# Sparse attention on one Trainium2 core: transposes in pairs, products with the values two groups behind, and a third place for cache pages

## What is computed

```python
# for each of 8 query heads (2 key heads g x 4 r), three softmaxes over their own keys
s_c = q . kc * scale + bias(rel_c);  p_c = masked_softmax(s_c);  o_c = p_c @ vc     # compressed blocks of 32 keys
imp = p_c.sum(heads of g) per block of 64;  idx = top_k(imp + forced, 16)            # which blocks are read
s_s = q . ks[idx] * scale + bias(rel_s);     p_s = masked_softmax(s_s);  o_s = p_s @ vs   # selected blocks
s_w = q . k * scale + bias(rel), window 512; p_w = masked_softmax(s_w);  o_w = p_w @ v    # window
o = gate_0 * o_c + gate_1 * o_s + gate_2 * o_w
```

## Time and profile before

| | us |
|---|---|
| median of 3 runs | 2830.55 |
| lowest, highest | 2830.36, 2838.09 |
| profiled execution, its own time | 2830.92 |
| profiled execution, span of its instructions | 2829.3 |
| PE busy in the span | 2645.5 (94%) |
| DVE, ACT, POOL busy | 1318.7, 856.8, 703.0 |
| granted clock of PE, mean | 0.958 |

### The profile page before, as it was taken

The page is one execution under the profiler, slowest core; times in us unless marked ns, Lnnn a source line. Parts: engine busy times, 40 slices in busy tenths (PEclk is TensorE's granted clock), DMA queues, the critical chain, the costliest instruction groups (busy, mean ns, idle before and its releaser), DMA issues. The chain is left out here.

```text
span 2829.3 us, 52704 instructions
## 1 busy us (share of the span) xinstructions
PE 2645.5 (94%) x21842; PEld 2424.8 (86%) x21842; DVE 1318.7 (47%) x2314; ACT 856.8 (30%) x1606; POOL 703.0 (25%) x554
## 2 busy tenths in 40 slices
PE   8999999999889987788879999999999999999997
PEld 8999999989767764455559899988999999999996
DVE  6999999213133456455553352334233323323234
ACT  5332202113222324565652222134221121120222
POOL 2222222222243420111203424201422222222222
PEclk9999999999877887999989999999999999999998
DMA  5122353332376625334316551233111111111112
GB/s 185 48 66 69 99 106 87 96 99 68 121 257 222 205 94 183 126 116 152 122 66 210 150 179 61 75 134 136 49 43 49 47 46 45 46 45 45 45 45 69
DMA packets 149345, 290.33 MB, mean 103 GB/s; under 512 B 28356, under 2 KB 97160, under 8 KB 146354
## 3 DMA queue, kind: packets, MB, share of 16 engines
q1 hardware_dynamic: 137586, 255.49, 28.5%
q0 software_dynamic: 11520, 31.47, 3.5%
HBM read 245.94 MB, written 51.93 MB: 105 GB/s over the span
## 5 line engine op out<-in xcount | busy, mean ns | idle before, releaser
L147 POOL TENSOR_TENSOR mlp_w_low<-mlp_w_raw,mlp_w_high 128x1024 fp32r<-128x1024 f32 x72 | 173.6, 2411 | 649.4 <-ACT mlp_w_high L143 649.4
L371 PE MATMUL in_psum<-x_high,in_w_high 128*128 128x352 f32 x1416 | 266.7, 330 | 21.4 <-DVE x_low L566 11.4
L147 POOL TENSOR_TENSOR in_w_low<-in_w_raw,in_w_high 128x1024 fp32r<-128x1024 f32 x59 | 147.9, 2506 | 546.8 <-ACT in_w_high L143 546.8
L2815 PE MATMUL mlp_psum<-mlp_in,mlp_w_high 128*128 128x352 f32 x1536 | 264.9, 324 | 0.0
L143 ACT ACTIVATE mlp_w_high<-mlp_w_raw 128x1024 fp32r<-128x1024 f32 x72 | 76.4, 1061 | 621.5 <-PE mlp_psum L2815 621.5
L371 PEld LDWEIGHTS in_psum<-x_high,in_w_high 128*128 128x128 f32 x1416 | 237.5, 192 | 29.6 <-issue 15.1
L371 PE MATMUL in_psum<-x_low,in_w_high 128*128 128x352 f32 x1416 | 260.3, 325 | 0.0
L371 PE MATMUL in_psum<-x_high,in_w_low 128*128 128x352 f32 x1416 | 259.6, 325 | 0.0
L2815 PEld LDWEIGHTS mlp_psum<-mlp_in,mlp_w_high 128*128 128x128 f32 x1536 | 251.2, 189 | 0.2
L371 PEld LDWEIGHTS in_psum<-x_low,in_w_high 128*128 128x128 f32 x1416 | 236.2, 190 | 0.0
L371 PEld LDWEIGHTS in_psum<-x_high,in_w_low 128*128 128x128 f32 x1416 | 235.4, 190 | 0.0
(11 more groups left out here) (483 smaller groups left out, 4439.9 us busy)
## 6 DMA issues: line engine op xcount, KB each, us to landing
mlp_w_raw<-in_w_mlp SPq DMA_DIRECT2D x64, 512.0 KB, 3.6
in_w_raw<-in_w_in SPq DMA_DIRECT2D x59, 512.0 KB, 4.2
nsa_ring<-in_cache_slc SPq DMA_DIRECT2D x144, 128.0 KB, 4.0
gdnp_page_ring<-in_cache_cmp POOLq DMA_DIRECT2D x128, 128.0 KB, 4.9
gdnp_page_ring<-in_cache_cmp SPq DMA_DIRECT2D x128, 128.0 KB, 5.8
u_scratch<-stage SPq DMA_DIRECT2D x28, 528.0 KB, 5.3
nsa_ring<-in_cache_slc POOLq DMA_DIRECT2D x112, 128.0 KB, 4.1
aux<-u_scratch SPq DMA_DIRECT2D x24, 528.0 KB, 3.9
```

Source lines behind the costliest of these rows:

```text
L147: self.nc.gpsimd.tensor_tensor(self.low[:, i % 2, 0:k * P], self.raw[:, i % 2, 0:k * P], self.high[:, i % 2, 0:k * P].bitcast(F32), ALU.su ...
L371: return mm(psum[:, e % 2, n, 0:WN], w[:, i % 2, c * P:(c + 1) * P], a[:, c, n * WN:(n + 1) * WN], start=x == 0 and c == 0, stop=x == 2 an ...
L2815: return mm(psum[:, e % 2, n, 0:WN], w[:, i % 2, c * P:(c + 1) * P], a(c)[:, column(n)], start=x == 0 and c == 0, stop=x == 2 and c == CHU ...
```

## The change

It touches only the sparse stage.

- The turned groups have two PSUM banks (`TBANKS` 2, banks 4 and 5) and still three slots in SBUF (`TSLOTS` 3). The result regions are two (`REGIONS` 2), each in a bank of its own (6 and 7).
- A piece of the tail is now two groups of an item: both are turned, then the values follow of all groups up to two behind the last one turned (`BEHIND`). A single group at an item's end is a piece of its own. The values so run over an item's end into the next item; ahead of loop step 6 (`RANKED`), which uses the result banks for the samples' block flags, and at the end of the loop they are brought up in full.
- ACT copies a result when the copy of the second group after the item's last one is done (`keep_result`), and no more at the item's end.
- DVE's `biases(i)` waits until item i - 4 is turned, and no more for its result.
- The ring has three places. The third lies over the tiles of the block ranking (3 of 4 samples) and over early constants (the fourth). Set j waits for the item of set j - 3; set 2, the first in the third place, for the end of the ranking (`flags_ready`).

```diff
-    HB, SETS, FIRST_SET = NB // 2, 2, 4
+    HB, SETS, FIRST_SET = NB // 2, 3, 4
-    SLOTS, TBANKS, REGIONS, LAG = 4, 3, 4, 3
+    SLOTS, TSLOTS, TBANKS, REGIONS, LAG = 4, 3, 2, 2, 3
+    BEHIND = 2
+    place_of_group = [(i, k) for i in range(NI) for k in range(len(groups(i)))]
+    ends_item = {first_group[i + 1] - 1: i for i in range(NI)}
...
-        pt = S("probs_t", [P, TBANKS, 4, P])
+        pt = S("probs_t", [P, TSLOTS, 4, P])
...
-        ring = alias("ring", [P, SETS, HB, 4, 2 * PAGE])
+        ring = alias("ring", [P, 2, HB, 4, 2 * PAGE])
+        third = nc.alloc_sbuf_tensor_at("nsa_ring_third", [P, HB - 1, 4, 2 * PAGE], F32, offset=ranking_at)
+        third_last = nc.alloc_sbuf_tensor_at("nsa_ring_third_last", [P, 4, 2 * PAGE], F32, offset=early.at)
+        set_pages = lambda j, b: ring[:, j % SETS, b] if j % SETS < 2 else third[:, b] if b < HB - 1 else third_last
...
-        O_BANK, M0, M1 = 7, 6, 7
-        region = lambda i: ps[:, O_BANK, i % REGIONS * P:(i % REGIONS + 1) * P]
+        O_BANK, M0, M1 = 6, 6, 7
+        region = lambda i: ps[:, O_BANK + i % REGIONS, 0:P]
...
             elif j == 0:
                 eng.wait_ge(v_turned, 2)
+            elif j == 1:
+                eng.wait_ge(spilled, 16)
             else:
-                eng.wait_ge(spilled, 16)
+                eng.wait_ge(flags_ready, 1)
...
-            def tail(i, step):
-                n = len(groups(i))
-                if step < n:
-                    turn(i, step)
-                if step >= 1:
-                    values(i, step - 1)
+            valued = [0]
+
+            def values_up_to(end):
+                while valued[0] < end:
+                    values(*place_of_group[valued[0]])
+                    valued[0] += 1
...
                 if i == RANKED:
+                    values_up_to(first_group[i - LAG])
                     pe.wait_ge(flags_ready, 1)
...
-                tailing = [(i - LAG, s) for s in range(len(groups(i - LAG)) + 1)] if i >= LAG else []
+                tailing = [(i - LAG, s) for s in range(0, len(groups(i - LAG)), 2)] if i >= LAG else []
                 for which, (n, k) in merged(scoring, tailing):
-                    (tail if which else score)(n, k)
+                    if which:
+                        pair = range(k, min(k + 2, len(groups(n))))
+                        for one in pair:
+                            turn(n, one)
+                        values_up_to(first_group[n] + pair[-1] + 1 - BEHIND)
+                    else:
+                        score(n, k)
+            values_up_to(first_group[NI])
...
                     next(exp_parts, None)
+                    if G - BEHIND in ends_item and ends_item[G - BEHIND] != RANKED - LAG - 1:
+                        keep_result(ends_item[G - BEHIND])
+                if i == RANKED - LAG - 1:
+                    keep_result(i)
                 for _ in exp_parts:
                     pass
+
+            def keep_result(i):
...
             def biases(i):
                 kind, r, tt = items[i]
                 if i >= SLOTS:
-                    dve.wait_ge(o_mm, i - SLOTS + 1)
+                    dve.wait_ge(pt_mm, first_group[i - SLOTS + 1])
```

More of the change, by code:

```diff
@@ L1641, in sparse @@
         strip = lambda b: slice(b * 32, (b + 1) * 32)
-        O_BANK, M0, M1 = 7, 6, 7
-        region = lambda i: ps[:, O_BANK, i % REGIONS * P:(i % REGIONS + 1) * P]
+        O_BANK, M0, M1 = 6, 6, 7
+        region = lambda i: ps[:, O_BANK + i % REGIONS, 0:P]
         sem = phase_semaphores(ctx, nc, "nsa_")
         loads = [sem("loads0"), sem("loads1")]
+        assert all(j % SETS == 0 for j in range(NS) if sets[j][0] == WIN)
         set_in, set_in_pool = [sem(f"set_in{s}") for s in range(SETS)], [sem(f"set_in_pool{s}") for s in range(SETS)]
@@ L1684, in load_set @@
             for (b, k), n in zip(places, numbers):
[L1685 removed]
+                eng.dma_start(set_pages(j, b)[:, k, :], t["cache_slc"][bass.DynSlice(n, 1), :, :].rearrange("a p n -> (a p) n")
                               ).then_inc(landed[j % SETS], 16)
@@ L1734, in score @@
                     for b in range(HB):
-                        last = mm(score_bank(G, 0)[strip(b), :], queries(sets[n][1], b), ring[:, n % SETS, b, :, 0:PAGE],
+                        last = mm(score_bank(G, 0)[strip(b), :], queries(sets[n][1], b), set_pages(n, b)[:, :, 0:PAGE],
                                   start=True, stop=True)
@@ L1781, in values @@
                         for b in range(HB):
-                            last = mm(region(i)[strip(b), :], pt[:, G % TBANKS, j, strip(b)], ring[:, n % SETS, b, j, PAGE:2 * PAGE],
+                            last = mm(region(i)[strip(b), :], pt[:, G % TSLOTS, j, strip(b)], set_pages(n, b)[:, j, PAGE:2 * PAGE],
                                       start=j == 0, stop=j == 3 and final)
@@ L1785, in values @@
                     x, hf, c = sets[n]
-                    last = mm(region(i), pt[0:NEW, G % TBANKS, 0, :], vn[:, hf, 0 if x == WIN else 1, :], start=False, stop=True)
+                    last = mm(region(i), pt[0:NEW, G % TSLOTS, 0, :], vn[:, hf, 0 if x == WIN else 1, :], start=False, stop=True)
                 else:
@@ L1792, in values @@
                             v = vc[0:w, dims] if x == CMP else vtok[:, 0 if x == SLC else 1, vb, dims]
-                            last = mm(region(i)[dims, :], v, pt[0:w, G % TBANKS, 2 * j + g, :], start=k == 0 and j == 0, stop=x == CMP)
+                            last = mm(region(i)[dims, :], v, pt[0:w, G % TSLOTS, 2 * j + g, :], start=k == 0 and j == 0, stop=x == CMP)
                 last.then_inc(o_mm if final else pv_mm, 1)
-            def tail(i, step):
-                n = len(groups(i))
-                if step < n:
-                    turn(i, step)
-                if step >= 1:
-                    values(i, step - 1)
+            valued = [0]
[3 more added lines that the diff above has]
+                    valued[0] += 1
             for c0, c1, b in ((0, BANK, 0), (BANK, NBIAS, 1)):
@@ L1897, in copies @@
                     act.wait_ge(pt_mm, G + 1)
-                    if G >= TBANKS:
-                        old = max(m for m in range(NI) if first_group[m] <= G - TBANKS)
-                        finished = G - TBANKS == first_group[old + 1] - 1
-                        act.wait_ge(*((o_mm, old + 1) if finished else (pv_mm, G - TBANKS - old + 1)))
+                    if G >= TSLOTS:
+                        old = max(m for m in range(NI) if first_group[m] <= G - TSLOTS)
+                        finished = G - TSLOTS == first_group[old + 1] - 1
+                        act.wait_ge(*((o_mm, old + 1) if finished else (pv_mm, G - TSLOTS - old + 1)))
                     if kind == SET:
@@ L1905, in copies @@
                         w, cols = (4 * (tt + 1), 2 * P) if group[0][0] == CMP else (P, 2 * P * len(group))
-                    act.activation(pt[0:w, G % TBANKS, :, :].rearrange("p a b -> p (a b)")[:, 0:cols], turn_bank(G)[0:w, 0:cols], ACT.Copy
+                    act.activation(pt[0:w, G % TSLOTS, :, :].rearrange("p a b -> p (a b)")[:, 0:cols], turn_bank(G)[0:w, 0:cols], ACT.Copy
                                    ).then_inc(pt_out, 1)
                     next(exp_parts, None)
+                    if G - BEHIND in ends_item and ends_item[G - BEHIND] != RANKED - LAG - 1:
+                        keep_result(ends_item[G - BEHIND])
+                if i == RANKED - LAG - 1:
+                    keep_result(i)
                 for _ in exp_parts:
                     pass
+            def keep_result(i):
+                kind, n, tt = items[i]
                 act.wait_ge(o_mm, i + 1)
@@ L1951, in _ @@
                         weights(hf)
+            for G in range(first_group[NI], first_group[NI] + BEHIND):
+                if G - BEHIND in ends_item:
+                    keep_result(ends_item[G - BEHIND])
             for hf in range(2):
```

5 lines of the change are left out of this document (4 added, 1 removed).

## The result

The changed kernel takes 2803.26 us (median of 4 runs, 2801.35 to 2806.72), against 2832.58 us for the kernel before in its runs beside it: a ratio of 0.9892, 95% interval 0.9874 to 0.991. That is 29 us less. Compared with the runs shown before the prediction, it is 27 us. The profiled execution took 2802.85 us, with a span of 2801.2 us. The last values of the main loop of the sparse stage end at 1444.7 us instead of 1473.5. The whole gain lies in it.

A forecast was written before the change was run, and what follows sets the result against it. The sparse loop was taken as bound by PE's work plus 57.1 us of PE waits. Terms -17 - 24 - 13 - 9 + 6 + 1.5 = -55.5 from 2830.9 gave 2775 us at the median; own range 2757 to 2790, all cases 2757 to 2806.

The forecast's parts named there:

- the ACT rival: In the sparse loop, ACT's copies at the two turn banks set the pace, adding 22 us waits: 2806 us; chance 0.20.
- Fewer changes of kind on PE: On PE in the sparse loop, fewer switches between turns, values and scores save 17 us, ends 9 and 19.
- Waits for copies: PE's waits for ACT's copies of turned groups fall from 35.6 to about 11.6 us: -24, ends -15 and -33.
- Pages: A third place for page sets in the sparse loop removes PE's waits for cache pages: -13 us, ends -7 and -14.
- Clock: Two thirds of the time PE loses at granted clock 0.5 in the loop is won back: -9 us, ends 0 and -14.
- Given back to DVE: PE's waits for DVE in the shorter loop double from 5.4 us: +6, ends 0 and +12.
- The values brought up ahead of step 6: Values brought up ahead of loop step 6 wait for two fresh copies, then the result copy waits: +1.5 us.
- the good ends: Low end of the forecast's own range, almost all favourable term ends together: -74.5 us, given as 2757 us.
- the third rival: In the loop, copies, banks and DVE merely trade places, waits stay, only page waits go: 2824 us; chance 0.03.
- copies: Sign in the loop: TensorE's waits for ACT's copies should be near 12 us.
- the value blocks: Sign on PE: two value blocks in a row should take about 1.0 us; 1.18 would refute the saving for values.
- The loop from first turns to last values: Sign: the sparse stage's main loop should last about 318 us; 365 or more would refute the mechanism of the waits.

The follow-up runs named there:

- single_pieces: The changed kernel with tail pieces of one group, so one turn and then values two groups behind; 2803.27 us, ratio 0.9889 to the kernel before.
- two_places: The changed kernel with the third place for page sets taken back; 2866.11 us, ratio 1.0105 to the kernel before.
- short_scales: The changed kernel with DVE multiplying only the first 32 columns of each softmax, the rest left unscaled; 2786.92 us, ratio 0.984 to the kernel before.
- scales_inside: The changed kernel with DVE's scales of item i - 2 after the second score chunk of item i; 2806.74 us, ratio 0.9907 to the kernel before.
- scores_early: The changed kernel with every score chunk 0.4 of its interval earlier among its step's tail pieces; 2809.22 us, ratio 0.9922 to the kernel before.
- copy_first: The changed kernel with no exponentials ahead of ACT's first copy of a step; 2811.73 us, ratio 0.9933 to the kernel before.
- scales_after_first: The changed kernel with DVE's scales of item i - 2 after the first score chunk of item i; 2796.73 us, ratio 0.9881 to the kernel before.

## Why the prediction was right or wrong

The direction and the range (2757 to 2806) held. The forecast did not: it said 55.5 us, and 29 came. That the range held is luck in part. 2803.26 us lies outside the forecast's own range (2757 to 2790) and inside the whole one only because it was stretched to the ACT rival, whose mechanism did not come. By the forecast's terms, in the loop from its first score:

1. *Fewer changes of kind on PE, -17.* The mechanism was right, and so was the choice between the two ends for values: two alike blocks cost as two turns do (1.03 us, not 1.18). PE's work fell from 305.6 us to 289.8, which is -15.8. The step from PE's work to the time held only in part: single_pieces gives the work back, and 7.3 of the 16.1 us go into PE's waits.
2. *Waits for copies, -24.* Measured -29.3, within the term's ends.
3. *Pages, -13.* Measured -8.5 in the change. The step "the release comes one set earlier, so even 7.0 us are covered" held for the release. "The values run about two groups later, some 2.5 us, which does not change that" holds with three places, but without the third it costs 58 us of waits (two_places): a set stands in its place for 30.3 us instead of 23.6. The 5.5 us that were left come from SP's list: it was looked through for what stands behind set 2, not for what stands ahead of set 5, where the loads of round 2 are.
4. *Clock, -9.* Measured +1.2 (22.3 us against 21.1). The lower clock had followed the waits for copies and pages, and the waits for DVE brought their own: the 3.59 us wait shown above ends inside a stretch (1271.3 to 1278.1). The term counted on most waits being gone.
5. *Given back to DVE, +6.* Measured +23.1. This is the term that was mis-sized, and with the clock the main error: 17 and 10 us of the 25 by which the loop missed. Its size was the 5.4 us of before, doubled, with the 71.5 us that DVE waits for scores read as room. DVE does not have that room at the time it is wanted: it waits in order for ACT's exponentials, ACT waits for its negmax, and PE for its banks. The terms taken off PE (1 to 3) were added as if nothing stood behind them.
6. *The values brought up ahead of step 6, +1.5.* Not seen: no values of the changed kernel wait for a copy, and the block flags wait 0.5 us for the result copy, where it was 1.2 before.

The sum of the measured terms: -15.8 - 29.3 - 8.5 + 1.2 + 23.1 - 0.7 = -30.0 us, of the 30.5 by which the loop is shorter. Two small slips do not matter to this: the good ends give 2756 us and not 2757, and the third rival's own numbers (-13, +6, +1.5) give 2825, not 2824.

Of its signs, copies (6.3 us, near 12 was said) and the value blocks came out as it wrote or better. The loop from first turns to last values (341.4 us against 318), PE's busy time in it (300.4 against 291), the pages (5.5 against 0 to 1), DVE (28.5 against 11) and the stretches at the lower clock (seven against three) did not.

The ACT rival named 2806 us, close to the time, but its mechanism was wrong. Turns wait 6.3 us for copies, not 22 more. The Trainium skill's page TensorEngine Tiling (Array Packing), section PSUM Bottleneck, was set beside it: after a fourfold speedup of TensorE by tiling the copy out of PSUM may bound. That fits only loosely: what bounds in part is DVE, which reads the scores out of PSUM, but also its work on SBUF (short_scales). By the same page of the Trainium skill, section Tiling Modes, a change of the tiling mode drains TensorE and a change of tile alone does not; the value blocks here agree (1.03 us for two of the same shape, against 2 x 0.59).

Shown: the waits moved to DVE, and less DVE work shortens the loop (short_scales). None of the four orders of the same work on PE, DVE or ACT did, as far as the ratios can tell (scales_inside, scores_early, copy_first, scales_after_first). What stays open is how much of the remaining 28.5 us is one closed round of PE, DVE and ACT and how much is single heavy steps such as the one with the samples' coefficients; no run separates these. No run takes work off ACT either, so its part in the round is read from the waits and not shown by an experiment.

## What to carry to other kernels

A wait that is taken off the busiest engine is only won up to the point where the engine that it waits for next is late, and an average busy share does not tell that point; follow, at a few places, what the next engine in line waits for itself. Where an order holds a buffer longer, count the time that one place is held (use, release, load) against the number of places: here the same change of order was 33 us slower with two places and 15 us faster with three, counted from the kernel with the same number of places. Fewer changes of kind on an engine that also waits elsewhere in each round show in full in its busy time and only in part in the kernel's. Before a difference between two traces is put down to a cause, count both from the same instruction and take idle time, the lower clock and work apart: here 11 us of spread lay ahead of the loop, and the clock moved the loop by 6 us and more between kernels.

## What was not expected of the hardware

The granted clock fell to 0.5 for 37.5 us in the loop although PE's idle share fell from 15% to 12%; two_places, where PE was busy for 317.8 of 406.3 us (22% idle), had 92 us at that level.
